# A decoder step: sample heads of the cross attention in four quarters of the PSUM rows, and row scalings of the delta rule moved from GpSimd to ScalarE and VectorE

## The reference

```python
k_beta = k * beta[..., None]
A = jnp.where(tri_strict, jnp.einsum('bnhid,bnhjd->bnhij', k_beta, k) * decay, 0.0)
rhs = jnp.concatenate([v * beta[..., None], k_beta * jnp.exp(gc)[..., None]], -1)
sol = lax.linalg.triangular_solve(jnp.eye(C) + A, rhs, left_side=True, lower=True)
u, w = sol[..., :dv], sol[..., dv:]
# scan over chunks
v_new = u_i - w_i @ S
o = (q_i * jnp.exp(gc_i)) @ S + qk_i @ v_new
S = S * jnp.exp(g_last) + (k_i * jnp.exp(g_last - gc_i)).T @ v_new
# afterwards, per head
o = o * lax.rsqrt(jnp.mean(jnp.square(o), -1) + RMS_EPS) * dn_norm_g * silu(dz)
```

```python
q = (x @ w_cq).reshape(B, L, X_HEADS, X_HEAD_DIM)
s = jnp.einsum('blhd,bmhd->bhlm', q, mem_k) * X_HEAD_DIM ** -0.5
p = jax.nn.softmax(s, -1)
o = jnp.einsum('bhlm,bmhd->blhd', p, mem_v)
return o.reshape(B, L, D_MODEL) @ w_co
```

## Time and profile before

| | |
|---|---|
| Device time, 3 runs | 2198.92 us median (2197.85 to 2202.18) |
| The profiled execution | 2201.09 us, of which the span is 2199.0 us |
| PE busy | 2093.6 us (95%) |
| DVE busy | 1641.5 us (75%) |
| ACT busy | 772.3 us (35%) |
| POOL busy | 559.6 us (25%) |

### The profile page before, as it was taken

The page is one execution under the profiler, slowest core; times in us unless marked ns, Lnnn a source line. Parts: engine busy times, 40 slices in busy tenths (PEclk is TensorE's granted clock), DMA queues, the critical chain, the costliest instruction groups (busy, mean ns, idle before and its releaser), DMA issues. The chain is left out here.

```text
span 2199.0 us, 33910 instructions
## 1 busy us (share of the span) xinstructions
PE 2093.6 (95%) x12934; PEld 1894.5 (86%) x12934; DVE 1641.5 (75%) x3051; ACT 772.3 (35%) x1237; POOL 559.6 (25%) x354
## 2 busy tenths in 40 slices
PE   8999978979999899999999999999989999999998
PEld 7998868868865699999999999999977777878776
DVE  5636657657143522899999979999979888898898
ACT  4335431232241132232234444444433333333332
POOL 0000042000000000031211125555536555665530
PEclk9999979989999999999999999999999999999999
DMA  5223210051343040486775758888899999999993
GB/s 164 78 97 112 82 45 1 31 186 58 120 144 129 13 154 1 135 293 226 269 242 196 246 171 334 336 333 334 337 367 385 387 387 377 387 388 386 385 367 120
DMA packets 223216, 483.75 MB, mean 220 GB/s; under 512 B 12015, under 2 KB 137199, under 8 KB 221446
## 3 DMA queue, kind: packets, MB, share of 16 engines
q1 hardware_dynamic: 177030, 314.56, 40.3%
q0 software_dynamic: 46080, 167.79, 21.0%
HBM read 423.29 MB, written 58.36 MB: 219 GB/s over the span
## 5 line engine op out<-in xcount | busy, mean ns | idle before, releaser
L2879 PE MATMUL ps<-v_high_low,gated_high_low 128*128 128x512 f32 x2304 | 534.0, 393 | 24.2 <-ACT gated_high_low L2947 21.8
L2879 PEld LDWEIGHTS ps<-v_high_low,gated_high_low 128*128 128x128 f32 x2304 | 433.5, 189 | 124.5 <-ACT v_high_low L2945 26.0
L2483 PE MATMUL ps<-x_high_low,u_high_low 128*128 128x384 f32 x1024 | 355.6, 347 | 0.2 <-ACT u_high_low L2549 0.2
L2484 PE MATMUL ps<-x_high_low,u_high_low 128*128 128x384 f32 x1024 | 345.0, 337 | 0.0
L2600 POOL DMA_INDIRECT scores<-peer_u,kept x64 | 95.1, 1486 | 781.3 <-DVE kept L2720 604.7
L2971 POOL DMA_INDIRECT outputs<-peer_v,kept x138 | 247.1, 1790 | 179.5 <-DVE kept L2988 146.5
L2558 ACT ACTIVATE kept<-ps 128x384 f32<-128x384 f32 x128 | 62.9, 491 | 407.9 <-PE ps L2488 407.9
L2488 PE MATMUL ps<-x_high_low,u_high_low 128*128 128x384 f32 x1024 | 204.7, 341 | 0.0
L2483 PEld LDWEIGHTS ps<-x_high_low,u_high_low 128*128 128x128 f32 x1024 | 192.5, 188 | 0.5 <-ACT u_high_low L2549 0.5
L2484 PEld LDWEIGHTS ps<-x_high_low,u_high_low 128*128 128x128 f32 x1024 | 192.8, 188 | 0.0
L3051 DVE TENSOR_TENSOR v_high_low<-raw_v,v_high_low 128x1024 fp32r<-128x1024 f32 x120 | 146.1, 1218 | 52.4 <-ACT v_high_low L2945 52.4
(11 more groups left out here) (453 smaller groups left out, 4257.7 us busy)
## 6 DMA issues: line engine op xcount, KB each, us to landing
experts<-peer_u SPq DMA_DIRECT2D x63, 1024.0 KB, 7.4
raw_v<-peer_v SPq DMA_DIRECT2D x60, 1024.0 KB, 15.1
hidden<-kept SPq DMA_DIRECT2D x64, 384.0 KB, 4.4
gates<-scores SPq DMA_DIRECT2D x12, 2048.0 KB, 9.5
first_hidden<-hidden SPq DMA_DIRECT2D x16, 768.0 KB, 16.8
outputs<-gates SPq DMA_DIRECT2D x16, 768.0 KB, 13.4
outputs<-hidden SPq DMA_DIRECT2D x16, 768.0 KB, 15.8
first_gates<-gates SPq DMA_DIRECT2D x15, 768.0 KB, 14.2
```

The lines of the kernel that those rows point to most:

```text
L2483: pe.matmul(o, utr[:, b, HI, k], xr[:, HI, k, 0:DN], start=(k == 0), stop=False)
L2484: pe.matmul(o, utr[:, b, HI, k], xr[:, LO, k, 0:DN], start=False, stop=False)
L2879: ins = pe.matmul(bank(c, 2 * t + h), gr[:, slot, x, DN * b + P * t:DN * b + P * t + P], vr[:, slot, y, D * b + 512 * h:D * b + 512 * h + ...
```

## The change

Cross attention, samples: the four heads no longer stand side by side in the columns of banks 6 and 7 on rows 0 to 31, but all in columns 0 to 255 of bank 6, head h on rows 32h to 32h+31 (`head_rows`). The matmuls of a batch go through the heads first and the two parts of the contraction second. Maxima, exponentials, division and the copy out then work on 128 rows at once, and the sample probabilities and outputs are turned by 2 full transposes each instead of 8 of 32 rows. Bank 7 becomes free, and the keys are turned in halves of 4 transposes that go round three banks (`key_bank`: 4, 5, 7), each copied out by one engine, ACT and DVE in turn.

Delta rule: q and k are turned ahead of the scaled rows (`turn_qk`, 8 transposes, right after the products of the tile before), the other two operands when `prepare` is done. Decayed keys and the values times beta go from POOL to ACT, as activations of 128 columns with the scale as a factor for each row (`decayed_keys` behind the exponentials of the next tile, `beta_values` in the first items of the inverse). The gains go to DVE (`gate_gains`, items 8 to 12 of the inverse). POOL keeps only the first level of the inverse. In the scan, `norm_tile(n)` moves from the end of step n into step n+1, behind the two subtractions.

```diff
-            for n in range(NT):
-                r = ROWS[n]
-                pe.wait_ge(prepared, n + 1)
-                for i, src in enumerate((ct[:, n, 0:512], ct[:, n, 512:1024], beta_k(n), qe)):
...
+            def turn_qk(n):
+                pe.wait_ge(unit_set, n + 1)
+                turn(n, ((2, ct[:, n, 0:512]), (3, ct[:, n, 512:1024]))).then_inc(turned_qk, 1)
...
+                turn(n, ((4, beta_k(n)), (5, qe))).then_inc(turned3, 1)
...
+                if n + 1 < NT:
+                    turn_qk(n + 1)
...
+            def keep_turned(n):
+                act.wait_ge(turned_qk, n + 1)
...
+                for i in range(2):
+                    act.copy(qkt[:, n % 2, i, 0:4 * r], bank(c, 2 + i, 4 * r))
+                act.wait_ge(turned3, n + 1)
+                act.copy(qkt[:, n % 2, 2, 0:4 * r], bank(c, 4, 4 * r)).then_inc(turned3_act, 1)
+
+            def decayed_keys(n):
+                act.wait_ge(exps, n + 1)
+                for h in range(DNH):
+                    act.activation(ct[0:r, n, P * h:P * h + P], beta_k(n)[0:r, P * h:P * h + P], ACT.Identity, scale=eg[0:r, n, h:h + 1])
+                for h in range(DNH):
+                    x = ct[0:r, n, 512 + P * h:640 + P * h]
+                    ins = act.activation(x, x, ACT.Identity, scale=eg[0:r, n, 4 + h:5 + h])
+                ins.then_inc(kg_set, 1)
...
+            for n in range(NT):
+                keep_turned(n)
+                if n + 1 < NT:
+                    row_exps(n + 1)
+                    decayed_keys(n)
...
+                if i == NT:
+                    decayed_keys(NT - 1)
+                elif i < NT - 1:
+                    beta_values(i)
...
                 update(i)
+                if GAINS_AT <= i < GAINS_AT + NT:
+                    gate_gains(i - GAINS_AT)
...
                 if n:
+                    norm_tile(n - 1)
                     norm_head(n - 1)
...
                     mask_k(n + 1)
-                    norm_tile(n)
...
-                pool.wait_ge(prepared, n + 1)
-                pool.wait_ge(turned3, n + 1)
-                rows(n, 0, eg, 0, beta_k(n)[0:r].rearrange("p (h k) -> p h k", h=4))
-                rows(n, 512, eg, 4).then_inc(kg_set, 1)
                 pool.wait_ge(at_set, n + 1)
...
-            for n in range(NT):
-                ins = rows(n, 1024, beta, 0)
-            ins.then_inc(bv_set, 1)
...
+    def head_rows(h):
+
+        return c.ps[SAMP * h:SAMP * h + SAMP, 512 * 6:512 * 6 + MEM]
...
+                for half in range(2):
+                    i = 4 * b + 2 * m + half
+                    if i < 3:
+                        pe.wait_ge(x_lo, x_no(3, 1) + 1)
+                    else:
+                        pe.wait_ge((k_out_act, k_out_dve)[(i - 3) % 2], (i - 3) // 2 + 1)
...
-            def score_keys(b, pair):
+            def score_keys(b, e):
...
+                for h in range(XH):
+                    ins = pe.matmul(head_rows(h), qm[:, b, 2 * h + e], kt[b % 2][:, 2 * h + e],
+                                    start=(b == 0 and e == 0), stop=(b == NB - 1 and e == 1), skip_group_check=True)
...
+                for m in range(2):
+                    for h in range(XH):
+                        ins = pe.matmul(head_rows(h), pm[:, b, XH * m + h], vs[b % 6][:, m, MEM * h:MEM * h + MEM],
+                                        start=(b == 0 and m == 0), stop=(b == NB - 1 and m == 1), skip_group_check=True)
```

More of the change, by code:

```diff
@@ L1074, in cumulate, with turn @@
                 ins.then_inc(cums, 1)
+            def turn(n, sources):
+                r = ROWS[n]
+                for o, src in sources:
+                    for h in range(DNH):
+                        ins = pe.transpose(bank(c, o)[:, r * h:r * h + r], src[0:r, P * h:P * h + P], ident[0:r, 0:r])
+                return ins
+            def turn_qk(n):
+                pe.wait_ge(unit_set, n + 1)
+                turn(n, ((2, ct[:, n, 0:512]), (3, ct[:, n, 512:1024]))).then_inc(turned_qk, 1)
             cumulate(0)
+            turn_qk(0)
             for n in range(NT):
@@ L1339, in update, with gate_gains @@
                 ins.then_inc(t_new, 1)
+            def gate_gains(n):
+                r = ROWS[n]
+                z = hd[0:r, n, 8:520].rearrange("p (h k) -> p h k", h=4)
+                if n == 0:
+                    v.wait_ge(gain_in, 16)
+                v.tensor_tensor(z, z, over(ng[0:r], 1, [r, 4, P]), ALU.mult).then_inc(gain_set, 1)
             mask_a(0)
@@ L1558, in phase_cross @@
     mx, sums = words(c, M_S + 2 * LayerNorm.SIZE, NT, 4), words(c, M_S + 2 * LayerNorm.SIZE + 20, NT, 4)
+    mxs, sums_s = mx[:, 4, 0:1], sums[:, 4, 0:1]
     scale = (D // XH) ** -0.5
@@ L1760, in turn_probs @@
                 for m in range(2):
-                    for h in range(XH):
-                        o = bank(c, 2 + m)[:, r * h:r * h + r] if n < 4 else bank(c, 4)[:, SAMP * (2 * h + m):SAMP * (2 * h + m) + SAMP]
-                        ins = pe.transpose(o, pr[0:r, n % 2, h, P * m:P * m + P], ident[0:r, 0:r])
+                    if n == 4:
+                        ins = pe.transpose(bank(c, 4)[:, P * m:P * m + P], prs[:, P * m:P * m + P], ident)
+                    else:
+                        for h in range(XH):
+                            ins = pe.transpose(bank(c, 2 + m)[:, r * h:r * h + r], pr[0:r, n % 2, h, P * m:P * m + P], ident[0:r, 0:r])
                 ins.then_inc(ptd, 1)
@@ L1839, in _ @@
                 pe.wait_ge(v_in[b], 16)
-                for h in range(XH):
-                    for m in range(2):
-                        ins = pe.matmul(bank(c, 6 + h // 2, 512, SAMP)[:, MEM * (h % 2):MEM * (h % 2) + MEM], pm[:, b, 2 * h + m],
-                                        vs[b % 6][:, m, MEM * h:MEM * h + MEM],
-                                        start=(b == 0 and h % 2 == 0 and m == 0), stop=(b == NB - 1 and m == 1), skip_group_check=True)
+                for m in range(2):
+                    for h in range(XH):
+                        ins = pe.matmul(head_rows(h), pm[:, b, XH * m + h], vs[b % 6][:, m, MEM * h:MEM * h + MEM],
+                                        start=(b == 0 and m == 0), stop=(b == NB - 1 and m == 1), skip_group_check=True)
                 ins.then_inc(v_used, 1)
@@ L1847, in _ @@
             pe.wait_ge(om_set, 1)
-            for ch in range(KD):
-                ins = pe.transpose(bank(c, 4)[:, SAMP * ch:SAMP * ch + SAMP], om[:, P * ch:P * ch + P], ident[0:SAMP, 0:SAMP])
+            for e in range(2):
+                ins = pe.transpose(bank(c, 4)[:, P * e:P * e + P], om[:, P * e:P * e + P], ident)
             ins.then_inc(om_turned, 1)
@@ L1913, in exps @@
                     act.wait_ge(ptd, n - 1)
+                if n == 4:
+                    act.activation(prs, bank(c, b0, MEM), ACT.Exp, bias=mxs, scale=scale, accum_out=sums_s).then_inc(expd, 1)
+                    return
                 for h in range(XH):
```

114 lines of the change are left out of this document (58 added, 56 removed).

## The result

The changed kernel takes 2139.05 us (median of 4 runs, 2136.83 to 2146.21), the kernel before 2199.94 on the same chip; the ratio is 0.9726 (0.9712 to 0.9739). The time is within 1.1 us of that of the rival "four at once", 2138. The profiled execution took 2141.16 us, its span is 2139.4, 59.6 less than before.

The account below looks back on a forecast made before the run. PE, busy 2093.6 of 2199.0 us, was taken as the bound. Savings of 18.0 (head), 4.6 (scan), 11.2 (keys), 13.7 (values) and 0.6 (small transposes) sum to 48.1, giving 2151 us; range 2140 to 2179.

Parts of the forecast that it names:

- four at once: Sample keys and values: all four quarters overlap, saving 17.2 and 20.1 us; whole kernel 2138 us; rival, chance 0.10.
- five units of eight: Sample keys and values: eight PE instructions take five units of 0.217 us, saving 11.2 and 13.7; main case, chance 0.60.
- slower: Sample keys and values: each change of quarter drains the array, up to 0.27 us each; 2211 us; rival, chance 0.04.
- POOL's stall: Start of the inverse: without POOL's work beside DVE's masks, first to third item takes 3.7 us, not 13.06; 9.4 saved.
- The ring: Head of delta phase: q and k leave the tile-to-tile chain, a round takes 6.15 us, four take 26.6; 7.1 saved.
- The end of the head: Delta phase, last transposes to first item of the inverse: 5.0 us in place of 7.5; 2.5 saved.
- ACT's activations: Head of delta phase: eight more per tile take 1.8 to 2.5 us; copies of turned keys at most 0.2 late.
- Scan: Normalisation moved behind the subtraction saves 1.53 us in each of three steps, 4.6 in all; ends 3.5 and 4.8.
- Third bank: Keys of the cross attention: turning by halves over three banks removes waits PE does not have in steady state; 0 saved.
- Gains and values times beta: Inverse: work moved to DVE and ACT costs nothing while covered; without cover the gains would cost 3.4 us.
- Waits that show once PE is faster: Keys and values, with all quarters overlapping: some 3.6 us for ACT's exponentials and copies, 0.7 for the seventh request's load.

Follow-up runs that it names:

- the delta part alone: The kernel before with only the delta rule's part of the change: 2176.05 us, ratio 0.9883 to the kernel before.
- four in a row: The changed kernel with the values' loop over heads outside that over key halves, four PE instructions running to one quarter: 2146.54 us, one run.
- the version with three edits: The changed kernel with gate sums read from PSUM, two exponentials ahead of ACT's key copy, half an output tile between value requests: 2130.19 us, ratio 0.9680.

## Why the prediction was wrong, step by step

- **The step that failed** is "If PE starts its instructions in order, the second half of head h and the first half of head h+1 run together and no more do", and with it "five units of eight". Eight take two units (0.57 us and not 1.2). A half that must wait for its own quarter doesn't hold up the halves behind it, as long as no more than three wait there; the order in the program has two in a row. The values then save 96 x 0.217 = 20.8 less waits, not 13.7, and the keys 19.2 instead of 11.2. These two terms are 11.5 us too small, and the whole miss is 12. The other bound had been worked out and came within 1 us (17.2 + 20.1 = 37.3 forecast for keys and values, 36.4 measured), in part by luck, since the keys saved 2.0 more than it says and the values 2.9 less. But it had a chance of 0.10 and the range was cut just above it, on an argument for which no row spoke. With both bounds open the range had to hold both. The Trainium skill (TensorE: Matmul & The Clock Gate, Part 3: Packing small matmuls) says that matmuls start and end in program order; these runs do not agree where the quarters differ: four start within 20 ns, though the program has two for each quarter one behind the other. The Trainium skill (TensorEngine Tiling (Array Packing), Theoretical Speedup) gives up to 4 times for outputs of at most 32 rows; 217 / 56 = 3.9 agrees.
- **Rival "slower"**: a change of quarter drains nothing. In the values a new quarter comes with every second instruction, at 56 ns each.
- **POOL's stall**: right in cause (the run with POOL's work back) and in place. 3.72 from the first to the third item, as worked out.
- **The ring**: right that q and k leave it; a round is 6.60 and not 6.15, since the copy L1324 now meets POOL's mask, +0.67 (6.2 with the copy from PSUM). The four rounds from 289.30 to 315.34 take 26.04 (26.6 forecast): the first, counted at 8.2 for its half clock, took 6.64. That is one execution's clock: the same code took 5.87 for it in the trace of the delta part alone and 7.96 in that of four in a row. The end of the head took 6.6 us instead of 5.0. Of these, 3.93 are the 20 transposes of the first level (L1118, 318.01 to 321.94) at a granted clock of 0.56; they took 4.15 before, at 0.50, and the forecast of 5.0 did not count them. PE waited for POOL's masks only 0.3 there. Errors of 0.6 and 1.6, and 1.0 that had been taken off for half clock in the items: the sum came out at 17.9 for 18.0, partly by luck.
- **ACT's activations**: eight take 2.35 us (1.8 to 2.5 forecast). The products wait 0.71 for a copy, not 0.2, but DVE, not the products, sets the round.
- **Scan**: 4.6 forecast, 4.6 measured, and shown by putting the edit back.
- **Third bank, "0"**: 0.5 a pair once the scores are short, 2.0 us in the keys by the traces, below what the whole time can show. **Gains and values times beta**: hidden, as forecast; the inverse is 0.5 longer.
- **Waits that show once PE is faster**: counted in the rival only. ACT's copies cost PE 2.3 us of the keys, by the version with three edits, and the loads of the seventh and eighth request 2.25 us and, with half clock behind them, 3.2. The rival had 0.7 for these loads: one lands 5.9 us after its issue (median, 5.0 before), and the eighth waits too.

## What to carry to other kernels

Small matmuls whose outputs use 32 rows run at once when neighbours in the program go to different quarters of the output rows; keep the runs for one quarter short (two or four here), and the time falls by the number of quarters. This is shown for float32 instructions of 128x256 alone. When PE gets four times faster in a stretch, read at once which loads and copies have to come four times faster, and put other work between them: here 3.2 of the 10.6 us that the values took were such waits and the half clock behind them. And before a difference of one or two microseconds between two traces is put down to an edit, compare a third trace of the same code: here the first pair of requests took 12.3 or 13.8 us by the clock alone. Last, an operation with both operands in SBUF on DVE should not run beside POOL's; moving one operand to PSUM frees it, but the next such operation may meet POOL instead.

## What the runs showed of the hardware that was not expected

- A quarter holds back the instructions behind it only from the fourth waiting one on: 57 ns an instruction with four in a row, 122 with eight, 180 with sixteen, and the second quarter's first starts 6 ns behind the thirteenth of sixteen and the fifth of eight.
- Weight loads of 106 to 110 ns (shortest and median of the values' own, as in the earlier trace rows) do not limit a pitch of 56 ns: loads for different quarters overlap too. All 128 together keep their part of PE busy for 4.03 us, where one behind the other they would take 13.6 or more.
- A copy of 128 x 4 elements from SBUF to SBUF took 0.84 us beside POOL and 0.17 without (0.16 from PSUM beside it): an instruction with one input was held up as well. The Trainium skill (SBUF — State Buffer, Who interferes with whom) names copies among the operations that can contend; it says that the one that comes second is blocked for the whole of the other, and this copy ended within 0.04 us of POOL's mask. A mask of 6.42 us, though, was held over five instructions of POOL and more, and ended while the row went on: at 327.07, 0.59 behind the start of POOL's ninth of ten, which took 1.71 us where the three before it took 1.25 or 1.26. The mask of 9.59 us in the kernel before ended in the same place, 0.58 behind the start of the ninth, which took 1.70. So it got in between two of POOL's instructions; why only there, no run shows.
